# A fourth tile of 512-column matmuls in the selection turns, and a new table that places 46 additions

## The chip, the cores and the metric

The kernel runs on one core of one Trainium2 chip. The metric is the device time of one execution in microseconds (us). Five engines work beside each other, each through its own list of instructions, and they meet at semaphores: TensorE (PE in the rows; PEld is its weight load), VectorE (DVE), ScalarE (ACT), GpSimd (POOL) and SyncE (SP), which here issues the DMAs.

## The reference, cut to what matters

One transformer-like block for 256 tokens of width 1024: three mixers (a state-space scan, block attention, retention), an output projection, and then a layer of 16384 experts with product keys. The change lies in the expert layer:

```python
q = (hf @ w_q).reshape(t, PEER_HEADS, 2, PEER_QDIM // 2)
sc = jnp.einsum('thcd,hcnd->thcn', q, sub_keys)
sv, si = lax.top_k(sc, PEER_TOPK)                  # the selection
fs, fp = lax.top_k(cand_s, PEER_TOPK)
gates = jax.nn.softmax(fs, axis=-1)
act = jax.nn.gelu(jnp.einsum('cd,chkd->chk', xc, ue))
out = jnp.einsum('chk,chkd->cd', gc * act, ve)
```

Each token picks 16 experts per head by two top-16 searches. The kernel computes the gelu of all 16384 experts for all 256 tokens instead of gathering, and then multiplies by gates that are zero for experts not picked.

## The kernel before, in words

**Tiles and turns.** The 16384 experts are 128 tiles of 128 experts. A turn has four tiles (`UN` = 4, called slots 0 to 3 here), so there are 32 turns of the first product (`keys_turn`) and then 32 of the second (`values_turn`). A tile (t, s) is slot s of turn t. Each tile of the first product contracts over 1024 = 8 blocks of 128 (two halves of four).

**Precision in halves.** Every float operand is split into a high part (fp32r) and a low part. ScalarE makes the high part of the weights (`w_hi<-raw`, L1673, two instructions of 512 columns per tile), GpSimd makes the low part (`w_lo<-raw,w_hi`, L1840, two per tile). Three products are wanted: high by high, high by low, low by high.

**Narrow and wide tiles.** A narrow tile makes the three products as three matmuls of 256 columns for each of the 8 blocks (`halves_product`, L450 to L452), all added up in one PSUM region. A wide tile joins the token operand's high and low parts side by side (`h_both`) and makes one matmul of 512 columns (L763) and one of 256 (L765, and L762 for the last block). Its PSUM bank then holds two halves that have to be added: ScalarE copies the second half to SBUF (`con<-ps`, L1720, called the copy below), VectorE adds it to the first (`ps<-ps,con`, L836, called the addition), and ScalarE applies the gelu (`acts<-ps`, L1702). A narrow tile has the gelu alone. Two PSUM banks are used in turns, so a tile can start only when the gelu of the tile two before it is done (`act_ready`).

**Which tiles are wide.** Turns 0, 1, 12, 13, 14 and all those after are wide in all slots (but for slot 3 of the last turn). Turns 2 to 11 are wide in slots 0 to 2 only (`WIDE_SEL`). These are the turns beside which VectorE does the selection.

**The selection on VectorE.** It consists of 286 steps, counted by `did`, in two passes of 133 steps (128 tokens each) and a softmax. A pass is: 16 MAX8, 32 searches and replacements, 16 MAX8 and 16 searches over 128 keys (steps 1 to 80), a CAST (L1280), a COPY, a sum of 2048 columns; 8 MAX8, 16 searches and replacements, 8 MAX8 and 8 searches (L1233) over 256 candidates (to step 123); then step 124, a subtraction of two SBUF tiles (L836, `routing<-routing`), 125 and 126, two TENSOR_SCALARs (L1289, L1290), 127, a CAST (L1292), and six operations of 2048 columns (steps 128 to 133). In the second pass 133 is to be added: L1289 is step 258, L1290 is 259, L1292 is 260.

**What sets the order.** Every engine works its list strictly in order. The order on VectorE is written by a table: after the steps named in `PART_STEPS` the next outstanding addition is put into VectorE's list (`next_part`). An addition that comes before its copy is done makes VectorE wait; one that comes after it makes ScalarE's gelu wait, and TensorE at last. After step 286 a copy of one column (L1322) tells TensorE that the gates are ready (`tok_ready`); TensorE waits for it after turn 13, ahead of the transposes of L794.

Of the kernel before, what the change touches and what calls it, by code (L numbers as in the profile page):

```python
# [67 lines left out]
UN = 4  # L68
# [3 lines left out]
G_TURN0 = TURNS - 1 - S // GT // UN  # L72
ROUTE_TURN = G_TURN0 - 1
EXP_TURN = G_TURN0 - 2
LOWEST = -3e38
WIDE_S, WIDE_SEL, WIDE_LAST = (0, 1, 2, 3), (0, 1, 2), (0, 1, 2)
SEL0, SEL1 = 2, EXP_TURN - 1
WIDE_TURNS = {0: 0, 1: 4, **{t: 8 + 3 * (t - SEL0) for t in range(SEL0, SEL1)}}
WIDE_TURNS |= {t: 8 + 3 * (SEL1 - SEL0) + UN * (t - SEL1) for t in range(SEL1, G_TURN0)}
WIDE_G0 = WIDE_TURNS[ROUTE_TURN] + UN  # L80
SEL_PARTS = [(t, s) for t in range(SEL0, ROUTE_TURN) for s in (WIDE_SEL if t < SEL1 else WIDE_S)]

PART_STEPS = (21, 30, 39, 62, 71, 80, 89, 95, 101, 115, 121, 126, 129, 130, 131, 135, 147, 156, 176, 185, 197, 215, 216, 223,
              236, 242, 249, 260, 261, 262, 264, 265, 266, 271, 276, 281)
WIDE_END = WIDE_G0 + S // GT

TWO_PI = 2 * np.pi
# [45 lines left out]
def build(nc, x, w_in, vecs, consts, rots, decay, mask, s5_b, s5_c, w_glu, w_out, w_q, keys, u_t, v, out, spill):  # L133
    with ExitStack() as ctx:
# [285 lines left out]
        def _(pe):  # L420
# [25 lines left out]
            def halves_product(dst, pairs, first, last):  # L446

                for i, (s_hi, s_lo, m_hi, m_lo) in enumerate(pairs):
                    end = last and i == len(pairs) - 1
                    pe.matmul(dst, s_hi, m_hi, start=first and i == 0, stop=False)  # L450
                    pe.matmul(dst, s_hi, m_lo, start=False, stop=False)  # L451
                    mm = pe.matmul(dst, s_lo, m_hi, start=False, stop=end)  # L452
                return mm
# [286 lines left out]
            def keys_turn(t, groups=None, first=False, first_group=False, wide=()):  # L740

                for s in range(UN):
                    if first and s == 0:
                        pe.wait_ge(scaled_ready, KC)
                    elif not (first and s < 2):
                        pe.wait_ge(act_ready, UN * t + s - 1)
                    for h in range(2):
                        if first and s == 0:
                            pe.wait_ge(th_ready, TH0 + 2 * KC + 4 * h + 4)
                            pe.wait_ge(tl_ready, TL0 + 2 * KC + 4 * h + 4)  # L750
                        pe.wait_ge(lo_ready, TAIL + 8 * t + 2 * s + h + 1)
                        slot = 2 * (s % 2) + h
                        pairs = [(w_hi[:, slot, k * P:(k + 1) * P], w_lo[:, slot, k * P:(k + 1) * P],
                                  h_hi[:, H2_PLACE[4 * h + k], :], h_lo[:, H2_PLACE[4 * h + k], :]) for k in range(4)]
                        if s not in wide:
                            halves_product(ps[:, s % 2, 0:S], pairs, h == 0, h == 1).then_inc(half_used, 1)
                            continue
                        for k, (s_hi, s_lo, m_hi, _) in enumerate(pairs):
                            both = h_both[:, H2_PLACE[4 * h + k]].rearrange("p a t -> p (a t)")
                            end = h == 1 and k == 3  # L760
                            if end:
                                pe.matmul(ps[:, s % 2, 0:S], s_lo, m_hi, start=False, stop=False)  # L762
                            mm = pe.matmul(ps[:, s % 2, :], s_hi, both, start=(h == 0 and k == 0), stop=end)  # L763
                            if not end:
                                mm = pe.matmul(ps[:, s % 2, 0:S], s_lo, m_hi, start=False, stop=False)  # L765
                        mm.then_inc(half_used, 1)
                    if groups is not None:
                        g = groups + s
                        pe.wait_ge(hot_ready, g + 1)
                        if not (first_group and s < 2):  # L770
                            pe.wait_ge(group_done, g - 1)
                        for q in range(GT):
                            mm = pe.matmul(ps[:, 4 + 2 * (s % 2) + q // 2, (q % 2) * 2 * NKEY:(q % 2 + 1) * 2 * NKEY],  # L773
                                           hot_j[:, s % 2, q, :], hot_gate[:, s % 2, q].rearrange("p a i -> p (a i)"),
                                           start=True, stop=True)
                        mm.then_inc(group_psum, 1)

            keys_turn(0, first=True, wide=WIDE_S)
            pe.wait_ge(keys_in, 16)
            pe.wait_ge(pq_ready, PH)  # L780
            key_scores(0)
            keys_turn(1, wide=WIDE_S)
            pe.wait_ge(sc_ready, 4)
            key_scores(1)
            with pe.Fori(2, EXP_TURN - 1) as t:
                keys_turn(t, wide=WIDE_SEL)
            pe.wait_ge(sc_ready, 8)
            keys_turn(EXP_TURN - 1, wide=WIDE_S)
            keys_turn(EXP_TURN, wide=WIDE_S)

            pe.wait_ge(tok_ready, 1)
            for t in range(TT):
                for a in range(3):
                    mm = pe.transpose(ps[:, 4 + t, a * P:(a + 1) * P], rows[:, t, a, :], ident)  # L794
            mm.then_inc(route_psum, 1)
            keys_turn(ROUTE_TURN, wide=WIDE_S)
            pe.wait_ge(route_low, TT)
            keys_turn(G_TURN0, groups=0, first_group=True, wide=range(UN))
            with pe.Fori(G_TURN0 + 1, TURNS - 1) as t:
# [27 lines left out]
        def _(dve):  # L827
# [115 lines left out]
            wide = lambda a: a.unsqueeze(2).to_broadcast([P, S5_T, 32])  # L943
# [304 lines left out]
                tt(ps[:, s % 2, 0:S], ps[:, s % 2, 0:S], low_out, ALU.add).then_inc(added, 1)  # L1248

            def add_parts(t):  # L1250
                for s in WIDE_S:
                    add_part(WIDE_TURNS[t] + s, s)

            queries(1)
# [4 lines left out]
            def next_part():  # L1259

                t, s = SEL_PARTS[sel_added[0]]
                add_part(WIDE_TURNS[t] + s, s)
                sel_added[0] += 1

            def did(ins):

                ch.did(ins)
                if ch.n - sel_first in PART_STEPS:
                    next_part()
# [52 lines left out]
            V.tensor_copy(top2[:, 0, 0:1], top2[:, 0, 1:2]).then_inc(tok_ready, 1)  # L1322
            while sel_added[0] < len(SEL_PARTS):
                next_part()
            add_part(WIDE_TURNS[ROUTE_TURN], 0)
            for t in range(TT):
# [3 lines left out]
            dve.wait_ge(route_low, TT)  # L1330
            add_part(WIDE_TURNS[ROUTE_TURN] + 1, 1)
            add_part(WIDE_TURNS[ROUTE_TURN] + 2, 2)
# [87 lines left out]
        def _(act):  # L1420
# [271 lines left out]
            def key_scores(t, b):  # L1692
                act.wait_ge(sc_psum, t + 1)
                A.activation(sc[:, t, b // 2, 4 * (b % 2):4 * (b % 2) + 4, :],
                             ps[:, 4 + b, :].rearrange("p (h n) -> p h n", h=4), ACT.Copy,
                             scale=rstd[:, t:t + 1]).then_inc(sc_ready, 1)
# [7 lines left out]
            def keys_turn(t, groups=None, first=False, first_group=False, extra=None, wide=(), wide_0=0, carried=None):  # L1704
                for s in range(UN):
                    n = UN * t + s
                    high(n + 1, (s + 1) % UN, t + (s + 1) // UN)
                    if extra is not None:
                        extra(s)
                    if groups is not None and not (first_group and s == 0):  # L1710
                        group_out(groups + s - 1, (s - 1) % 2)
                    if s == 0 and carried is not None:
                        act.wait_ge(added, carried)
                        gelu(t - 1, UN - 1, first)
                    if s - 1 in wide:
                        act.wait_ge(added, wide_0 + s)
                        gelu(t, s - 1, first)
                    act.wait_ge(half_used, TAIL + 2 * n + 2)
                    if s in wide:
                        A.activation(low_out, ps[:, s % 2, S:2 * S], ACT.Copy).then_inc(part_ready, 1)  # L1720
                    else:
                        gelu(t, s, first)

            def wide_turn(t, **how):
                after = WIDE_TURNS[t] if t in (1, EXP_TURN, ROUTE_TURN) else None
                keys_turn(t, wide=WIDE_S, wide_0=WIDE_TURNS[t], carried=after, **how)

            def group_out(g, b):

# [9 lines left out]

            wide_turn(0, first=True, extra=last_queries)  # L1740
            wide_turn(1, extra=lambda s: key_scores(0, s))
            keys_turn(2, extra=lambda s: key_scores(1, s), wide=WIDE_SEL, wide_0=WIDE_TURNS[SEL0], carried=WIDE_TURNS[1] + UN)
            with act.Fori(3, EXP_TURN - 1) as t:
                keys_turn(t, wide=WIDE_SEL, wide_0=3 * t + (WIDE_TURNS[SEL0] - 3 * SEL0))
            wide_turn(EXP_TURN - 1)

            def route_rows(s):
# [15 lines left out]
            with act.Fori(G_TURN0 + 1, TURNS - 1) as t:  # L1763
                keys_turn(t, groups=UN * t - UN * G_TURN0, wide=range(UN), wide_0=UN * t + (WIDE_G0 - UN * G_TURN0),
                          carried=UN * t + (WIDE_G0 - UN * G_TURN0))
# [149 lines left out]
```

## Time and profile before

| | us |
|---|---|
| median of 3 runs | 901.53 |
| lowest and highest | 901.40, 901.64 |
| the profiled execution | 901.37 |
| its span, first to last instruction | 899.6 |

The profiled execution is 0.16 us from the median. Between its span and its time lie 1.8 us that no instruction of the profile fills. The page gives the busy time of each engine as a share of the span; the chain says which engine's work, followed back from the last instruction, the end hung on. TensorE's granted clock is 1.0 (the upper level, 2.4 GHz) in all slices. The selection turns lie at about 180 to 294 us.

### The profile page before, as it was taken

The numbers are of one execution on the slowest core, as the hardware profiler recorded it, in microseconds if no ns is written. First come the engines' busy times: TensorE is split into PE (matmuls) and PEld (weight loads), VectorE is DVE, ScalarE is ACT, GpSimd is POOL, SyncE is SP. The second block draws the span as 40 slices with busy tenths as digits, with TensorE's granted clock in tenths as the row PEclk, the third lists the DMA queues.
The fourth block names the chain that finished last, engine by engine and source line by source line (L and its number), as shares of the span: only waits on it lengthen the run. The fifth ranks groups of instructions, "written<-read, shape, count | busy, mean of one in ns | idle before, by whom it ended". The sixth has DMA issues, their size and how long they took to land.

```text
span 899.6 us, 18356 instructions
## 1 busy us (share of the span) xinstructions
PE 891.8 (99%) x4842; PEld 761.1 (85%) x4842; DVE 744.5 (83%) x1697; ACT 576.9 (64%) x1182; POOL 426.4 (47%) x342
## 2 busy tenths in 40 slices
PE   8999999999999999999999999999999999999998
PEld 5877888899999888888888888888888888888886
DVE  7979535199999859999999988888888888888886
ACT  7759566665555567777777776565656565655563
POOL 5875288889999987777777772000000000000000
PEclk9999999999999999999999999999999999999999
DMA  9835050566666665555565657766667677666663
GB/s 335 296 108 188 1 211 23 197 204 231 232 233 231 229 221 207 202 199 209 189 219 186 216 184 262 246 236 235 244 243 244 238 243 244 233 240 247 242 239 128
DMA packets 67755, 191.52 MB, mean 213 GB/s; under 512 B 6672, under 2 KB 8592, under 8 KB 67728
## 3 DMA queue, kind: packets, MB, share of 16 engines
q1 hardware_dynamic: 67440, 191.09, 60.6%
q8 instruction: 13, 0.21, 0.1%
q10 hardware_dynamic: 288, 0.10, 0.0%
q14 instruction: 14, 0.11, 0.0%
HBM read 173.86 MB, written 17.30 MB: 212 GB/s over the span
## 4 chain that ended last, share of the span: by engine, by line
PE 94%; DVE 3%; DMA 1%; ACT 0%; SPq 0%; issue 0%; DVEq 0%
PE ps L763 24%; PE ps L450 16%; PE ps L451 16%; PE ps L452 16%; PE ps L765 11%; PE ps L773 3%; PE ps L717 2%; PE ps L762 2%; DMA routing<-in_w_in 1%; DVE ps L836 1%; PE ps L719 1%; DVE routing L836 1%; DVE ps L1014 1%; PE ps L736 0%; PE ps L611 0%; PE ps L442 0%
## 5 line engine op out<-in xcount | busy, mean ns | idle before, releaser
L1673 ACT ACTIVATE w_hi<-raw 128x512 fp32r<-128x512 f32 x512 | 308.2, 628 | 136.1 <-PE ps L452 135.3
L1840 POOL TENSOR_TENSOR w_lo<-raw,w_hi 128x512 fp32r<-128x512 f32 x256 | 327.1, 1300 | 67.2 <-ACT w_hi L1673 66.4
L763 PE MATMUL ps<-h_both,w_hi 128*128 128x512 f32 x936 | 331.5, 394 | 0.0
L765 PE MATMUL ps<-h_both,w_lo 128*128 128x256 f32 x819 | 229.4, 280 | 0.0
L836 DVE TENSOR_TENSOR w_lo<-raw,w_hi 128x512 fp32r<-128x512 f32 x256 | 177.3, 693 | 57.1 <-ACT w_hi L1673 41.8
L763 PEld LDWEIGHTS ps<-h_both,w_hi 128*128 128x128 f32 x936 | 173.8, 188 | 31.1 <-issue 0.2
L450 PE MATMUL ps<-w_hi,hot_gate 128*128 128x512 f32 x512 | 199.2, 389 | 0.0
L452 PE MATMUL ps<-w_hi,hot_gate 128*128 128x512 f32 x512 | 199.2, 389 | 0.0
L451 PE MATMUL ps<-w_lo,hot_gate 128*128 128x512 f32 x512 | 199.2, 389 | 0.0
L765 PEld LDWEIGHTS ps<-h_both,w_lo 128*128 128x128 f32 x819 | 154.7, 189 | 1.1
L1720 ACT ACTIVATE con<-ps 128x256 f32<-128x256 f32 x117 | 45.0, 385 | 108.4 <-PE ps L763 108.4
L450 PEld LDWEIGHTS ps<-w_hi,hot_gate 128*128 128x128 f32 x512 | 96.1, 188 | 20.1
L451 PEld LDWEIGHTS ps<-w_lo,hot_gate 128*128 128x128 f32 x512 | 96.1, 188 | 19.9
L452 PEld LDWEIGHTS ps<-w_hi,hot_gate 128*128 128x128 f32 x512 | 96.1, 188 | 19.9
L1805 POOL TENSOR_TENSOR w_lo<-routing,w_hi 128x512 fp32r<-128x512 f32 x72 | 91.9, 1297 | 40.2 <-ACT w_hi L1440 39.2
L1352 DVE SCALAR_TENSOR_TENSOR hot_gate<-ps,route_t 128x256 fp32r<-128x256 f32 x256 | 105.6, 475 | 0.0
L836 DVE TENSOR_TENSOR route_t<-acts,routing 128x256 f32<-128x256 f32 x128 | 81.3, 635 | 0.0
L836 DVE TENSOR_TENSOR ps<-ps,con 128x256 f32<-128x256 f32 x117 | 49.9, 426 | 37.8 <-ACT con L1720 37.2
L1702 ACT ACTIVATE acts<-ps 128x256 f32<-128x256 f32 x128 | 48.8, 381 | 20.4 <-PE ps L452 11.7
L836 DVE TENSOR_TENSOR routing<-routing,ps 128x512 f32 (+3 forms) x74 | 51.3, 700 | 11.8 <-ACT routing L1679 6.1
L1440 ACT ACTIVATE w_hi<-routing 128x512 fp32r<-128x512 f32 x70 | 42.6, 628 | 22.9 <-PE ps L452 19.6
L1770 ACT ACTIVATE hot_gate<-route_t 128x256 fp32r<-128x256 f32 x128 | 53.5, 418 | 2.3 <-DVE route_t L836 2.3
(242 smaller groups left out, 1090.2 us busy)
## 6 DMA issues: line engine op xcount, KB each, us to landing
raw<-in_u_t SPq DMA_DIRECT2D x128, 512.0 KB, 4.0
raw<-in_v SPq DMA_DIRECT2D x128, 512.0 KB, 3.3
act_spill<-acts SPq DMA_DIRECT2D x62, 256.0 KB, 2.2
acts<-act_spill SPq DMA_DIRECT2D x62, 256.0 KB, 3.4
routing<-in_w_in SPq DMA_DIRECT2D x4, 2048.0 KB, 11.9
routing<-in_w_out SPq DMA_DIRECT2D x2, 2048.0 KB, 7.6
routing<-in_w_q SPq DMA_DIRECT2D x2, 2048.0 KB, 7.7
routing<-in_w_in SPq DMA_DIRECT2D x2, 1024.0 KB, 10.7
```

The lines of the kernel that those rows point to most:

```text
L450: pe.matmul(dst, s_hi, m_hi, start=first and i == 0, stop=False)
L451: pe.matmul(dst, s_hi, m_lo, start=False, stop=False)
L452: mm = pe.matmul(dst, s_lo, m_hi, start=False, stop=end)
L763: mm = pe.matmul(ps[:, s % 2, :], s_hi, both, start=(h == 0 and k == 0), stop=end)
L765: mm = pe.matmul(ps[:, s % 2, 0:S], s_lo, m_hi, start=False, stop=False)
L836: return V.tensor_tensor(out_, a, b, op)
L1352: ins = V.scalar_tensor_tensor(hot_gate[:, s % 2, q], iota_p.unsqueeze(1).to_broadcast([P, 2, NKEY]), route_t[:, 0, one], route_t[:, 2:4, ...
L1673: A.activation(w_hi[:, 2 * (s % 2) + h, :], raw[:, s, h * HALF:(h + 1) * HALF], ACT.Copy)\
L1702: A.activation(acts[:, s, :], ps[:, s % 2, 0:S], ACT.Gelu_apprx_tanh).then_inc(act_ready, 1)
L1770: A.activation(a_hi[:, s, :], weighted[:, s % 2, :], ACT.Copy).then_inc(wh_ready, 1)
L1805: G.tensor_tensor(w_lo[:, m % 4, :], w_ring[n % W_SLOTS][:, k, :], w_hi[:, m % 4, :].bitcast(F32), ALU.subtract).then_inc(lo_ready, 1)
L1840: G.tensor_tensor(w_lo[:, slot, :], raw[:, s, h * HALF:(h + 1) * HALF], w_hi[:, slot, :].bitcast(F32), ALU.subtract).then_inc(lo_ready, 1)
```

## The change

Slot 3 of turns 2 to 11 becomes wide. TensorE's `keys_turn` and ScalarE's `keys_turn` get all four slots, ScalarE carries the gelu of slot 3 into the next turn as it did in the all-wide turns, and VectorE gets ten more additions. With them the list of additions during the selection grows from 38 to 48, of which the table places 46 (36 before); the last two follow the selection's end as before.

```diff
-WIDE_S, WIDE_SEL, WIDE_LAST = (0, 1, 2, 3), (0, 1, 2), (0, 1, 2)
+WIDE_LAST = (0, 1, 2)
-SEL_PARTS = [(t, s) for t in range(SEL0, ROUTE_TURN) for s in (WIDE_SEL if t < SEL1 else WIDE_S)]
+SEL_PARTS = [(t, s) for t in range(SEL0, ROUTE_TURN) for s in range(UN)]
-PART_STEPS = (21, 30, 39, 62, 71, 80, ..., 115, 121, 126, 129, 130, 131, 135, ..., 249, 260, 261, 262, 264, ..., 276, 281)
+PART_STEPS = (21, 31, 40, 49, 61, 71, ..., 114, 120, 127, 128, 129, 130, 131, 132, 134, ..., 254, 258, 261, 262, 263, ..., 277, 282)
...
             with pe.Fori(2, EXP_TURN - 1) as t:
-                keys_turn(t, wide=WIDE_SEL)
+                keys_turn(t, wide=range(UN))
...
             with act.Fori(3, EXP_TURN - 1) as t:
-                keys_turn(t, wide=WIDE_SEL, wide_0=3 * t + (WIDE_TURNS[SEL0] - 3 * SEL0))
+                keys_turn(t, wide=range(UN), wide_0=UN * t, carried=UN * t)
```

The lines of the new kernel are numbered 1 to 2 lower than those of the old one (L836 becomes L835, L763 becomes L762).

On TensorE, in the loop over turns 3 to 11, the second half of slot 3 reads before (L450 to L452 are the three products of a narrow tile, `h_both` the token operand):

```order
L450 MATMUL ps<-h_both,w_hi 128x256
L451 MATMUL ps<-h_both,w_hi 128x256
L452 MATMUL ps<-h_both,w_lo 128x256
L450 MATMUL ps<-h_both,w_hi 128x256
L451 MATMUL ps<-h_both,w_hi 128x256
L452 MATMUL ps<-h_both,w_lo 128x256
```

and now, at the same place:

```order
L762 MATMUL ps<-h_both,w_hi 128x512
L764 MATMUL ps<-h_both,w_lo 128x256
L762 MATMUL ps<-h_both,w_hi 128x512
L764 MATMUL ps<-h_both,w_lo 128x256
L762 MATMUL ps<-h_both,w_hi 128x512
L764 MATMUL ps<-h_both,w_lo 128x256
```

Three matmuls of 256 columns per block became one of 512 and one of 256.

On VectorE, the end of the first pass (steps 115 to 130) before; MAX_INDEX is the search, `ps<-ps,con` an addition:

```order
215 L836 TENSOR_TENSOR ps<-ps,con 128x256
216 L1233 MAX_INDEX routing<-routing 128x8 x6
217 L836 TENSOR_TENSOR ps<-ps,con 128x256
218 L1233 MAX_INDEX routing<-routing 128x8 x2
219 L836 TENSOR_TENSOR routing<-routing 128x128
220 L1289 TENSOR_SCALAR routing<-routing 128x128
221 L1290 TENSOR_SCALAR routing<-routing 128x128
222 L836 TENSOR_TENSOR ps<-ps,con 128x256
223 L1292 CAST routing<-routing 128x256
224 L836 TENSOR_TENSOR ps<-routing,ps 128x2048
225 L836 TENSOR_TENSOR routing<-ps,routing 128x2048
226 L836 TENSOR_TENSOR ps<-ps,con 128x256
```

and now:

```order
222 L835 TENSOR_TENSOR ps<-ps,con 128x256
223 L1232 MAX_INDEX routing<-routing 128x8 x3
224 L835 TENSOR_TENSOR routing<-routing 128x128
225 L1288 TENSOR_SCALAR routing<-routing 128x128
226 L1289 TENSOR_SCALAR routing<-routing 128x128
227 L1291 CAST routing<-routing 128x256
228 L835 TENSOR_TENSOR ps<-ps,con 128x256
229 L835 TENSOR_TENSOR ps<-routing,ps 128x2048
230 L835 TENSOR_TENSOR ps<-ps,con 128x256
231 L835 TENSOR_TENSOR routing<-ps,routing 128x2048
```

The addition of tile (5, 2) stood ahead of the CAST and now stands behind it, and there is an addition behind each of the 2048-column operations that follow.

On VectorE, the same place of the second pass before:

```order
306 L836 TENSOR_TENSOR ps<-ps,con 128x256
307 L1233 MAX_INDEX routing<-routing 128x8 x7
308 L836 TENSOR_TENSOR routing<-routing 128x128
309 L1289 TENSOR_SCALAR routing<-routing 128x128
310 L1290 TENSOR_SCALAR routing<-routing 128x128
311 L1292 CAST routing<-routing 128x256
312 L836 TENSOR_TENSOR ps<-ps,con 128x256
313 L836 TENSOR_TENSOR ps<-routing,ps 128x2048
314 L836 TENSOR_TENSOR ps<-ps,con 128x256
```

and now:

```order
318 L835 TENSOR_TENSOR ps<-ps,con 128x256
319 L1232 MAX_INDEX routing<-routing 128x8 x2
320 L835 TENSOR_TENSOR routing<-routing 128x128
321 L1288 TENSOR_SCALAR routing<-routing 128x128
322 L835 TENSOR_TENSOR ps<-ps,con 128x256
323 L1289 TENSOR_SCALAR routing<-routing 128x128
324 L1291 CAST routing<-routing 128x256
325 L835 TENSOR_TENSOR ps<-routing,ps 128x2048
326 L835 TENSOR_TENSOR ps<-ps,con 128x256
```

The addition of tile (11, 0) moved from behind the CAST to between the two TENSOR_SCALARs, and the one of tile (10, 3) (row 318) is new.

## Rows read from the trace of the kernel before

**Rows 1.** Page, part 1 (busy us, share of span, instructions) and part 4 (chain)

```profile
PE 891.8 (99%) x4842; PEld 761.1 (85%) x4842; DVE 744.5 (83%) x1697; ACT 576.9 (64%) x1182; POOL 426.4 (47%) x342
...
PE 94%; DVE 3%; DMA 1%; ACT 0%; SPq 0%; issue 0%; DVEq 0%
```

**Rows 2.** Table by stage: turns 2-11, turn 12 (start:end width, busy us per engine)

```profile
183.44:296.54 113.10, 113.10 (x722) 102.47 (x721) 109.38 (x417) 68.09 (x153) 101.21 (x80) 1.00 0.68 232
296.54:307.77 11.23, 11.23 (x65) 9.86 (x65) 9.56 (x16) 6.79 (x16) 10.21 (x9) 1.00 0.64 212
```

**Rows 3.** Timeline, TensorE: start us, length us, line, operation; narrow slot 3 of turn 2

```profile
189.09 0.28 PE L450 MATMUL ps<-h_both,w_hi 128*128 128x256 f32 x1
189.21 0.28 PE L451 MATMUL ps<-h_both,w_hi 128*128 128x256 f32 x1
...
191.97 0.40 PE L763 MATMUL ps<-h_both,w_hi 128*128 128x512 f32 x1
192.20 0.28 PE L765 MATMUL ps<-h_both,w_lo 128*128 128x256 f32 x1
192.32 0.40 PE L763 MATMUL ps<-h_both,w_hi 128*128 128x512 f32 x1
```

**Rows 4.** Waits, 180 to 316 us: total us, times, longest us

```profile
POOL w_lo L1840 <- ACT w_hi L1673: 14.2, 40, 2.4
...
DVE ps L836 <- ACT con L1720: 4.3, 14, 0.7
```

**Rows 5.** Timeline, TensorE, last matmul of a tile and first of the next

```profile
197.35 0.63 PE L763 MATMUL ps<-h_both,w_hi 128*128 128x512 f32 x2
```

**Rows 6.** Timeline, ScalarE, copies, weight splits and gelus

```profile
197.78 0.39 ACT L1720 ACTIVATE con<-ps 128x256 f32<-128x256 f32 x1 [1.09 <-PE ps L763]
...
220.38 0.39 ACT L1720 ACTIVATE con<-ps 128x256 f32<-128x256 f32 x1 [1.13 <-PE ps L763]
...
223.16 0.38 ACT L1720 ACTIVATE con<-ps 128x256 f32<-128x256 f32 x1 [1.09 <-PE ps L763]
...
228.85 0.38 ACT L1720 ACTIVATE con<-ps 128x256 f32<-128x256 f32 x1 [1.25 <-PE ps L763]
229.13 1.15 ACT L1673 ACTIVATE w_hi<-raw 128x512 fp32r<-128x512 f32 x2
230.62 0.38 ACT L1702 ACTIVATE acts<-ps 128x256 f32<-128x256 f32 x1 [0.34 <-DVE ps L836]
```

**Rows 7.** Timeline, GpSimd

```profile
221.36 2.60 POOL L1840 TENSOR_TENSOR w_lo<-raw,w_hi 128x512 fp32r<-128x512 f32 x2 [0.28 <-ACT w_hi L1673]
224.15 2.59 POOL L1840 TENSOR_TENSOR w_lo<-raw,w_hi 128x512 fp32r<-128x512 f32 x2 [0.19 <-ACT w_hi L1673]
...
283.82 5.19 POOL L1840 TENSOR_TENSOR w_lo<-raw,w_hi 128x512 fp32r<-128x512 f32 x4 [0.47 <-ACT w_hi L1673]
...
311.82 2.60 POOL L1840 TENSOR_TENSOR w_lo<-raw,w_hi 128x512 fp32r<-128x512 f32 x2 [0.25 <-ACT w_hi L1673]
```

**Rows 8.** Timeline, VectorE, end of the first pass

```profile
220.79 0.43 DVE L836 TENSOR_TENSOR ps<-ps,con 128x256 f32<-128x256 f32 x1
221.14 0.08 DVE L1233 MATCH_VALUE_LOAD routing<-routing 128x8 f32 x1
...
221.54 0.07 DVE L1233 MATCH_VALUE_LOAD routing<-routing 128x8 f32 x1
...
222.05 0.76 DVE L836 TENSOR_TENSOR routing<-routing 128x128 f32<-128x128 f32 x1
222.73 1.31 DVE L1289 TENSOR_SCALAR routing<-routing 128x128 uint32<-128x128 uint32 x1
223.97 0.21 DVE L1290 TENSOR_SCALAR routing<-routing 128x128 uint32<-128x128 uint32 x1
224.10 0.42 DVE L836 TENSOR_TENSOR ps<-ps,con 128x256 f32<-128x256 f32 x1
224.44 1.15 DVE L1292 CAST routing<-routing 128x256 f32<-128x256 uint32 x1
225.62 2.30 DVE L836 TENSOR_TENSOR ps<-routing,ps 128x2048 f32<-128x2048 f32 x1
227.96 2.29 DVE L836 TENSOR_TENSOR routing<-ps,routing 128x2048 f32<-128x2048 f32 x1
230.16 0.42 DVE L836 TENSOR_TENSOR ps<-ps,con 128x256 f32<-128x256 f32 x1
```

**Rows 9.** Timeline, VectorE, the same place of the second pass

```profile
283.46 0.29 DVE L836 TENSOR_TENSOR routing<-routing 128x128 f32<-128x128 f32 x1
283.67 0.22 DVE L1289 TENSOR_SCALAR routing<-routing 128x128 uint32<-128x128 uint32 x1
283.80 0.22 DVE L1290 TENSOR_SCALAR routing<-routing 128x128 uint32<-128x128 uint32 x1
284.06 1.27 DVE L1292 CAST routing<-routing 128x256 f32<-128x256 uint32 x1
```

**Rows 10.** Timeline, VectorE, end of the selection, and TensorE's transposes behind it

```profile
313.19 1.38 DVE L836 TENSOR_TENSOR routing<-routing 128x128 f32<-128x128 f32 x1
314.61 0.15 DVE L1322 COPY routing<-routing 128x1 f32<-128x1 f32 x1
...
316.25 0.82 PE L794 MATMUL ps<-con,routing 128*128 128x128 f32 x6
```

More of the change, by code:

```diff
@@ L75 @@
 LOWEST = -3e38
-WIDE_S, WIDE_SEL, WIDE_LAST = (0, 1, 2, 3), (0, 1, 2), (0, 1, 2)
+WIDE_LAST = (0, 1, 2)
 SEL0, SEL1 = 2, EXP_TURN - 1
-WIDE_TURNS = {0: 0, 1: 4, **{t: 8 + 3 * (t - SEL0) for t in range(SEL0, SEL1)}}
-WIDE_TURNS |= {t: 8 + 3 * (SEL1 - SEL0) + UN * (t - SEL1) for t in range(SEL1, G_TURN0)}
+WIDE_TURNS = {t: UN * t for t in range(G_TURN0)}
 WIDE_G0 = WIDE_TURNS[ROUTE_TURN] + UN
-SEL_PARTS = [(t, s) for t in range(SEL0, ROUTE_TURN) for s in (WIDE_SEL if t < SEL1 else WIDE_S)]
-PART_STEPS = (21, 30, 39, 62, 71, 80, 89, 95, 101, 115, 121, 126, 129, 130, 131, 135, 147, 156, 176, 185, 197, 215, 216, 223,
-              236, 242, 249, 260, 261, 262, 264, 265, 266, 271, 276, 281)
+SEL_PARTS = [(t, s) for t in range(SEL0, ROUTE_TURN) for s in range(UN)]
+PART_STEPS = (21, 31, 40, 49, 61, 71, 80, 83, 88, 95, 101, 107, 114, 120, 127, 128, 129, 130, 131, 132, 134, 146, 156, 165,
+              175, 184, 197, 206, 214, 216, 222, 228, 235, 241, 248, 254, 258, 261, 262, 263, 264, 265, 266, 272, 277, 282)
 WIDE_END = WIDE_G0 + S // GT
@@ L776, in keys_turn @@
                         mm.then_inc(group_psum, 1)
-            keys_turn(0, first=True, wide=WIDE_S)
+            keys_turn(0, first=True, wide=range(UN))
             pe.wait_ge(keys_in, 16)
@@ L781, in _ @@
             key_scores(0)
-            keys_turn(1, wide=WIDE_S)
+            keys_turn(1, wide=range(UN))
             pe.wait_ge(sc_ready, 4)
@@ L785, in _ @@
             with pe.Fori(2, EXP_TURN - 1) as t:
-                keys_turn(t, wide=WIDE_SEL)
+                keys_turn(t, wide=range(UN))
             pe.wait_ge(sc_ready, 8)
-            keys_turn(EXP_TURN - 1, wide=WIDE_S)
-            keys_turn(EXP_TURN, wide=WIDE_S)
+            keys_turn(EXP_TURN - 1, wide=range(UN))
+            keys_turn(EXP_TURN, wide=range(UN))
             pe.wait_ge(tok_ready, 1)
@@ L795, in _ @@
             mm.then_inc(route_psum, 1)
-            keys_turn(ROUTE_TURN, wide=WIDE_S)
+            keys_turn(ROUTE_TURN, wide=range(UN))
             pe.wait_ge(route_low, TT)
@@ L1250, in add_parts @@
             def add_parts(t):
-                for s in WIDE_S:
+                for s in range(UN):
                     add_part(WIDE_TURNS[t] + s, s)
@@ L1724, in wide_turn @@
             def wide_turn(t, **how):
-                after = WIDE_TURNS[t] if t in (1, EXP_TURN, ROUTE_TURN) else None
-                keys_turn(t, wide=WIDE_S, wide_0=WIDE_TURNS[t], carried=after, **how)
+                keys_turn(t, wide=range(UN), wide_0=WIDE_TURNS[t], carried=WIDE_TURNS[t] if t else None, **how)
             def group_out(g, b):
@@ L1741, in _ @@
             wide_turn(1, extra=lambda s: key_scores(0, s))
-            keys_turn(2, extra=lambda s: key_scores(1, s), wide=WIDE_SEL, wide_0=WIDE_TURNS[SEL0], carried=WIDE_TURNS[1] + UN)
+            keys_turn(2, extra=lambda s: key_scores(1, s), wide=range(UN), wide_0=WIDE_TURNS[SEL0], carried=WIDE_TURNS[1] + UN)
             with act.Fori(3, EXP_TURN - 1) as t:
-                keys_turn(t, wide=WIDE_SEL, wide_0=3 * t + (WIDE_TURNS[SEL0] - 3 * SEL0))
+                keys_turn(t, wide=range(UN), wide_0=UN * t, carried=UN * t)
             wide_turn(EXP_TURN - 1)
```

## The prediction

> **What bounds the kernel now.** I read the busy shares and the chain first [rows 1]: TensorE is busy for 99% of the span and holds 94% of the chain, so the end moves with TensorE's list alone, by what its instructions cost and by what it is made to wait. Then I read the table by stage for the stretch that the change touches [rows 2]: over the ten selection turns TensorE is busy in all of the 113.10 us, so before the change it never waits there. VectorE (109.38) and GpSimd (101.21) are nearly as full. The view of waits [rows 4] says what VectorE has to spare: it waits 14 times, 4.3 us in all, for ScalarE's copy, and GpSimd waits 40 times, 14.2 us in all, for the split weights, about once per tile. So TensorE is the bound, VectorE runs at its pace with some 4 us of slack, and what can go wrong is an addition that comes too late.
>
> **What TensorE gains.** The columns are the same: 24 matmuls of 256 columns are 6144, 8 of 512 and 8 of 256 are 6144 as well. What differs is the spacing. In the narrow tile matmuls start 0.12 us apart (189.09, 189.21), and the tile takes 191.97 - 189.09 = 2.88 us [rows 3]. In the wide one a pair starts every 0.35 us (191.97 to 192.32), 8 x 0.35 = 2.80. By stages: the ten turns with one narrow tile take 113.10 / 10 = 11.31 us, the all-wide turn 12 takes 11.23, which is 2.81 a tile [rows 2]. The difference is 0.08 a turn, ten times: **-0.8 us**. The bounds are -0.7 (2.88 less 2.81) and, if each of the 80 weight loads that vanish freed all of its time, -12.6: the loads are busy for 761.1 us over 4842 of them [rows 1], 0.157 each. Matmuls that start 0.12 us apart [rows 3] while a load takes more than that show that the loads overlap, so I take -0.8.
>
> **What the other engines get.** ScalarE gets ten copies of 0.38 us (3.8 us; it is busy 68.09 of 113.10 us [rows 2], and its order in slot 3 becomes that of the slots before it). VectorE gets ten additions, each holding its list for 0.35 us (220.79 to 221.14 [rows 8]): 3.5 us, less than the 4.3 us of waits, so as a sum they fit. The last additions and the end of the selection stay within their slack: VectorE's signal at 314.61 lasts to 314.76, TensorE comes to L794 at 316.25 [rows 10], 1.5 us later. The last placed addition, of tile (13, 1), moves one step later, and its tile comes earlier with TensorE, so this slack stays. DMAs don't change; the results of slots 2 and 3 are stored somewhat later in the turn, since the gelu of slot 3 now follows the next turn's first split; the waits of this stretch are for engines, none of the large ones for a DMA. What decides is each addition's place.
>
> **How late an addition may be.** Let c be the start of a tile's copy. The copy takes 0.39 us and the addition can start 0.03 us behind it, at c + 0.42. ScalarE then splits the next weights; the gelu starts 0.46 us after the addition's start if that is later (230.16 to 230.62) and takes 0.38, so it ends 0.84 us after the addition's start [rows 6, 8]. The tile's last matmul starts at c - 0.43 (197.35 against 197.78) and the next tile's first 0.24 later, at c - 0.19 [rows 5, 6]. The tile after that reuses the bank and wants to start at c - 0.19 + 2.81 = c + 2.62. So the addition must start by c + 1.78, 1.36 us after it could; each microsecond beyond it is one on TensorE. The latest before is at 230.16 for the copy of 228.85, which is 0.89 us behind c + 0.42 [rows 6, 8], and TensorE did not wait.
>
> **What makes VectorE late.** Three operations at the end of a pass take far longer in one place than in the other: the subtraction 0.76 against 0.29 us, L1289 1.31 against 0.22, and the CAST 1.15 and 1.27 [rows 8, 9]. Beside GpSimd's rows the reason shows: GpSimd's pair of 221.36 consists of two operations of 1.30 us. The subtraction of 222.05 ends when the first does (222.66), L1289 ends when the second does (223.96), L1290 at 223.97 falls into GpSimd's gap and takes 0.21, and the CAST ends just after 224.15 + 1.30 = 225.45. In the second pass the subtraction, L1289 and L1290 all start before 283.82, when GpSimd starts again, and are short; the CAST of 284.06 ends with GpSimd's operation [rows 7, 9]. The 1.38 us of the product at 313.19 end with the pair of 311.82 too [rows 7, 10]. So these forms wait for GpSimd's operation in progress, and where GpSimd has its next one ready, one such form passes between two of GpSimd's. GpSimd's pair starts at c + 0.98 (221.36 against 220.38), its first operation ends at c + 2.28, the pair at c + 3.58, and the next pair starts at c + 2.81 + 0.98 = c + 3.79: the gap is 0.2 us.
>
> The Trainium skill ("SBUF — State Buffer", section "Who interferes with whom") states the same as a lock: VectorE with two SBUF inputs, or in a two-port mode (copy, cast, tensor_scalar), and GpSimd exclude each other for whole instructions. Without that rule nothing speaks against the new table and the sum would be -0.8; with it the two stalls below are to be added. The trace agrees with it at the four places just read.
>
> **First pass, tile (5, 2).** Let c be the copy of tile (5, 1). Its addition is now behind step 120, at c + 0.42. VectorE goes on at c + 0.77, three searches follow (0.40, 0.40 and 0.51 by the starts 221.14, 221.54, 222.05 [rows 8]), and the subtraction is asked for at c + 2.08: before c + 2.28, so it ends there, L1289 ends at c + 3.58, L1290 starts at c + 3.59 in the gap. The CAST follows 0.26 later (283.80 to 284.06 [rows 9]), at c + 3.85. GpSimd has started at c + 3.79. So the CAST ends at about c + 5.1, and the addition of (5, 2), which stood ahead of it before and now stands behind it, starts at c + 5.2. Its limit is c + 2.81 + 1.78 = c + 4.59: **+0.6 us**. Behind it two 2048-column operations of 2.20 us (227.96 to 230.16 [rows 8]), each with an addition of 0.35, run at 2.55 a tile against 2.81, so the lateness falls by 0.26 a tile and costs nothing more.
>
> **Second pass, tile (11, 1).** Let c be the copy of tile (10, 3). Addition at c + 0.42, two searches, subtraction asked for at c + 0.77 + 0.40 + 0.51 = c + 1.68, inside GpSimd's first operation. It ends at c + 2.28, L1289 at c + 3.58. The addition of (11, 0) is now here: c + 3.59 to c + 3.94, which covers the gap. L1290 comes at c + 3.94, GpSimd started at c + 3.79: L1290 ends at c + 5.09, and the CAST behind the second operation at c + 6.39. The 2048-column comparison starts 0.17 later (225.45 to 225.62 [rows 7, 8]) and takes 2.20, so the addition of (11, 1) starts at c + 8.76. Its limit is c + 5.62 + 1.78 = c + 7.40: **+1.4 us**. Before, the three forms fell ahead of GpSimd's start, and the addition ahead of this comparison.
>
> No row shows TensorE held by a gelu, so what a restart costs can't be read. I bound it by 0 and by the 0.19 us from a tile's end to ScalarE's copy, the same kind of release the other way round [rows 5, 6], and take 0, since TensorE's next matmul stands ready in its list; the two stalls could thus be 0.4 longer in all.
>
> **The sum.** -0.8 + 0.6 + 1.4 = +1.2 us, against the profiled execution 901.37 + 1.2 = 902.6, against the median 901.53 + 1.2 = 902.7. I forecast **902.7 us**. A difference under 0.2% (1.8 us) is about what a measurement of this kernel can tell from no change, and by that this is no change.
>
> **The rivals.**
>
> *No stall: 900.7 us.* The holds by GpSimd don't fall as worked out, and TensorE keeps its 0.8 us. For it: TensorE is never held before, with one addition already 0.89 us late, and VectorE's holds vary between passes. Against it: GpSimd's gap is 0.2 us in 2.8, so a form that it holds rarely misses it.
>
> *One stall only: 901.3 to 902.1 us.* -0.8 + 0.6 = -0.2, if L1290 slips ahead of GpSimd in the second pass, by 0.15 us: then one hold goes, the limit is overrun by some 0.1 to 0.3 and the sum is -0.8 + 0.6 + 0.3 = +0.1 at most, 901.3 to 901.6. Or -0.8 + 1.4 = +0.6 if the CAST of the first pass slips ahead by its 0.06 us: 902.1.
>
> *Slower, by a hold more: 904.0 us.* In the first pass L1290 has to be in GpSimd's gap, 0.2 us wide. If the subtraction comes 0.2 us later than worked out (after c + 2.28), it takes the place of L1289, L1289 that of L1290, and L1290 misses the gap. Then another 1.30 us is put on the addition of (5, 2): the stall is 1.9, the sum -0.8 + 1.9 + 1.4 = +2.5. It decides from that 0.2 us on. For it: three more additions ahead of this point, of tiles (2, 3), (3, 3) and (4, 3), each 0.35 us of VectorE's time. Against it: VectorE waits for the copy of nearly every tile and so starts afresh.
>
> *The wide tile saves more than its spacing: under 899.7 us.* Weight loads would have to be what TensorE is short of; the 0.12 us spacing speaks against it.
>
> **How the numbers follow.** Forecast 0.48; no stall 0.18; one stall only 0.16; a hold more 0.14; more saved 0.04. The forecast, no stall and one stall lie within 0.2% of before, 0.82, of which I give 0.02 to the outer sides. Faster 0.05, same 0.80, slower 0.15. The range goes from 900.6, just below the case without a stall, to 904.0, the case with one hold more; outside are the larger gain and half of the slow case, some 0.15.
>
> **What would show it.** In the profile after: the windows of ten turns at 11.23 us each but for two longer ones; the matmuls of slot 3 at 0.35 a pair; a wait of TensorE for the gelu ahead of tile (6, 0), some 0.6 us, and ahead of (11, 3), some 1.4 us; the last CAST of each pass, and in the second pass both TENSOR_SCALARs, at some 1.2 us; no wait ahead of the transposes. The prediction is wrong if TensorE isn't held in these turns, or is held at other tiles, or if the ten turns' matmuls cost more or less than 11.15 to 11.30 a turn without a wait.

## The result and the profile after

| | median us | lowest to highest | runs |
|---|---|---|---|
| before | 901.19 | 900.58 to 901.64 | 15 |
| changed | 902.89 | 902.51 to 903.80 | 15 |

The ratio is 1.0021, with a 95% interval from 1.0014 to 1.0028: the change costs 1.7 us (1.2 were forecast, 902.7 us). The forecast held such a difference too small to tell from no change; fifteen runs of each kernel do tell it.

The page of the changed kernel, parts 1 and 4, answers to [rows 1]:

```profile
PE 891.7 (99%) x4762; PEld 756.7 (84%) x4762; DVE 749.6 (83%) x1707; ACT 579.3 (64%) x1192; POOL 426.2 (47%) x342
...
PE 88%; DVE 10%; ACT 1%; DMA 1%; issue 0%; POOL 0%; SPq 0%; DVEq 0%
```

80 matmuls are gone, as counted, and TensorE is as busy as before in all. What is new is that the chain which ended last now runs over VectorE for 10% of the span, not 3%. It enters VectorE's list at two additions and follows it back from there, from 226.0 to 218.5 us and from 292.3 to 244.6 us. This says where to look, in the selection turns, but not what VectorE costs there: the share is far more than the 1.7 us at stake.

The table by stage, with the ten selection turns in the first row (from the boundary of slots 0 and 1 of turn 2 to that of turn 12, as in [rows 2]) and turn 12 in the second:

```profile
184.13:298.91 114.78, 112.94 (x641) 98.24 (x641) 113.27 (x427) 71.04 (x163) 101.10 (x80) 1.00 0.68 227
298.91:310.11 11.20, 11.20 (x66) 9.83 (x65) 10.76 (x18) 6.79 (x16) 10.20 (x9) 1.00 0.74 234
```

The ten turns take 114.78 us against 113.10, so 1.68 us more, and TensorE, busy in all of it before, is now idle for 1.8 us of it. This matches the medians' 1.7. The two profiled spans differ by 2.3 us (901.9 against 899.6), because the profiled execution of the changed kernel took 903.73 us, 0.84 above its median; the other 0.69 lies before turn 2, which begins anywhere between 183.1 and 184.5 us in the nine profiles of this study, whatever the edit. So from here on the ten turns are the meter: they don't see what happens at the start. Each such number is one profile. How far it can be trusted is not measured by itself; two kernels that should not differ in it, before and before with the indices in PSUM, have 113.10 and 113.08.

TensorE's waits in the stretch are two. Its timeline around the first, ahead of tile (6, 0), and around the second, ahead of (11, 3); in brackets the idle time and what ended it:

```profile
226.08 0.39 PE L762 MATMUL ps<-h_both,w_hi 128*128 128x512 f32 x1
227.00 0.49 PE L762 MATMUL ps<-h_both,w_hi 128*128 128x512 f32 x1 [0.53 <-ACT acts L1701]
227.34 0.28 PE L764 MATMUL ps<-h_both,w_lo 128*128 128x256 f32 x1
227.45 0.40 PE L762 MATMUL ps<-h_both,w_hi 128*128 128x512 f32 x1
...
291.58 0.39 PE L762 MATMUL ps<-h_both,w_hi 128*128 128x512 f32 x1
293.28 0.49 PE L762 MATMUL ps<-h_both,w_hi 128*128 128x512 f32 x1 [1.31 <-ACT acts L1701]
293.61 0.28 PE L764 MATMUL ps<-h_both,w_lo 128*128 128x256 f32 x1
```

The brackets say 0.53 and 1.31, less than is lost. Matmuls of 512 columns start 0.24 us apart from tile to tile, here 0.92 and 1.70: that is 0.68 and 1.46. The first pair after each wait takes 0.45 instead of 0.35 (227.00 to 227.45). So each wait costs 0.1 more: 0.78 and 1.56, together 2.34 us. From 113.10 + 2.34 = 115.44 to 114.78 the wide tiles then give back 0.66.

What ended the waits is ScalarE's gelu, started late; its copies of tiles (5, 1) and (10, 3), from which the prediction counts, are the first row of each pair:

```profile
220.88 0.39 ACT L1719 ACTIVATE con<-ps 128x256 f32<-128x256 f32 x1 [1.09 <-PE ps L762]
...
226.49 0.38 ACT L1701 ACTIVATE acts<-ps 128x256 f32<-128x256 f32 x1 [1.37 <-DVE ps L835]
...
283.59 0.39 ACT L1719 ACTIVATE con<-ps 128x256 f32<-128x256 f32 x1 [1.12 <-PE ps L762]
...
292.77 0.38 ACT L1701 ACTIVATE acts<-ps 128x256 f32<-128x256 f32 x1 [2.15 <-DVE ps L835]
```

The view of waits also has one of 1.6 us of the weight load ahead of (11, 3), put down to GpSimd's low parts. But GpSimd's pair before it ends at 290.18 + 2.52 = 292.70, and the load starts at 293.28 with the matmul: the gelu, done at 293.15, came last there.

VectorE and GpSimd at the first place. VectorE in the end of the first pass, to be read against [rows 8]:

```profile
221.30 0.43 DVE L835 TENSOR_TENSOR ps<-ps,con 128x256 f32<-128x256 f32 x1
...
222.95 0.35 DVE L835 TENSOR_TENSOR routing<-routing 128x128 f32<-128x128 f32 x1
223.22 1.32 DVE L1288 TENSOR_SCALAR routing<-routing 128x128 uint32<-128x128 uint32 x1
224.46 0.21 DVE L1289 TENSOR_SCALAR routing<-routing 128x128 uint32<-128x128 uint32 x1
224.70 1.41 DVE L1291 CAST routing<-routing 128x256 f32<-128x256 uint32 x1
226.04 0.42 DVE L835 TENSOR_TENSOR ps<-ps,con 128x256 f32<-128x256 f32 x1
```

GpSimd in the same stretch:

```profile
221.86 2.59 POOL L1838 TENSOR_TENSOR w_lo<-raw,w_hi 128x512 fp32r<-128x512 f32 x2 [0.23 <-ACT w_hi L1672]
224.68 2.57 POOL L1838 TENSOR_TENSOR w_lo<-raw,w_hi 128x512 fp32r<-128x512 f32 x2 [0.23 <-ACT w_hi L1672]
```

The CAST asks at 224.70, 0.02 us after GpSimd has started its next pair. It lasts 1.41 us, to 226.11, about the end of GpSimd's first instruction at 224.68 + 1.30 = 225.98, and the addition behind it starts at 226.04. The addition before all this, at 221.30, starts 0.03 us behind the end of its copy (220.88 + 0.39 = 221.27): VectorE had not fallen behind up to there. The same holds in the second pass (284.01 against 283.98).

VectorE at the same place of the second pass, to be read against [rows 9]:

```profile
284.01 0.43 DVE L835 TENSOR_TENSOR ps<-ps,con 128x256 f32<-128x256 f32 x1
...
285.26 0.89 DVE L835 TENSOR_TENSOR routing<-routing 128x128 f32<-128x128 f32 x1
286.07 1.32 DVE L1288 TENSOR_SCALAR routing<-routing 128x128 uint32<-128x128 uint32 x1
287.32 0.42 DVE L835 TENSOR_TENSOR ps<-ps,con 128x256 f32<-128x256 f32 x1
287.65 1.11 DVE L1289 TENSOR_SCALAR routing<-routing 128x128 uint32<-128x128 uint32 x1
288.79 1.28 DVE L1291 CAST routing<-routing 128x256 f32<-128x256 uint32 x1
290.11 2.30 DVE L835 TENSOR_TENSOR ps<-routing,ps 128x2048 f32<-128x2048 f32 x1
292.31 0.43 DVE L835 TENSOR_TENSOR ps<-ps,con 128x256 f32<-128x256 f32 x1
```

GpSimd beside it:

```profile
284.72 5.20 POOL L1838 TENSOR_TENSOR w_lo<-raw,w_hi 128x512 fp32r<-128x512 f32 x4 [0.41 <-ACT w_hi L1672]
```

Its four instructions end at 286.02, 287.32, 288.62 and 289.92, and the four forms end at 286.15, 287.39, 288.76 and 290.07: one behind each. The subtraction and the two TENSOR_SCALARs took 0.29, 0.22 and 0.22 before and are now all held; the CAST was held before too (1.27). The addition of tile (11, 1) starts at 292.31, 2.7 us after its copy (289.20 to 289.59) is done.

The wait ahead of the transposes did not come: they start at 318.60, and VectorE's signal is issued at 316.97.

### The profile page after: what moved, and what is told of

It reads as the page before. It is cut to its first block, busy times and chain, and to the rows that moved or that the text cites. A ratio compares the mean times of both kernels' runs of the same rounds, so it can differ in the third digit from the quotient of the medians.

```text
span 901.9 us, 18129 instructions
## 1 busy us (share of the span) xinstructions
PE 891.7 (99%) x4762; PEld 756.7 (84%) x4762; DVE 749.6 (83%) x1707; ACT 579.3 (64%) x1192; POOL 426.2 (47%) x342
## 4 chain that ended last, share of the span: by engine, by line
PE 88%; DVE 10%; ACT 1%; DMA 1%; issue 0%; POOL 0%; SPq 0%; DVEq 0%
PE ps L762 22%; PE ps L449 15%; PE ps L450 15%; PE ps L451 15%; PE ps L764 10%; PE ps L772 3%; DVE ps L835 2%; PE ps L716 1%; PE ps L761 1%; DVE routing L1232 1%; DVE routing L835 1%; DVE routing L1225 1%; DVE routing L1226 1%; DMA xs<-in_x 1%; DVE routing L1229 1%; PE ps L718 1%
## 5 line engine op out<-in xcount | busy, mean ns | idle before, releaser
L762 PE MATMUL ps<-h_both,w_hi 128*128 128x512 f32 x1016 | 357.7, 395 | 1.8 <-ACT acts L1701 1.8
L764 PE MATMUL ps<-h_both,w_lo 128*128 128x256 f32 x889 | 249.1, 280 | 0.0
L835 DVE TENSOR_TENSOR w_lo<-raw,w_hi 128x512 fp32r<-128x512 f32 x256 | 177.3, 693 | 54.0 <-ACT w_hi L1672 39.5
L762 PEld LDWEIGHTS ps<-h_both,w_hi 128*128 128x128 f32 x1016 | 187.5, 188 | 36.2 <-POOL w_lo L1838 1.6
L450 PE MATMUL ps<-w_lo,hot_gate 128*128 128x512 f32 x512 | 199.2, 389 | 0.0
L764 PEld LDWEIGHTS ps<-h_both,w_lo 128*128 128x128 f32 x889 | 167.9, 189 | 1.9
L1719 ACT ACTIVATE con<-ps 128x256 f32<-128x256 f32 x127 | 48.8, 385 | 113.4 <-PE ps L762 113.4
L450 PEld LDWEIGHTS ps<-w_lo,hot_gate 128*128 128x128 f32 x512 | 96.1, 188 | 19.8
L835 DVE TENSOR_TENSOR route_t<-acts,routing 128x256 f32<-128x256 f32 x128 | 81.3, 635 | 3.2 <-PE ps L451 2.7
L835 DVE TENSOR_TENSOR ps<-ps,con 128x256 f32<-128x256 f32 x127 | 53.9, 424 | 34.4 <-ACT con L1719 34.2
L835 DVE TENSOR_TENSOR routing<-routing,ps 128x512 f32 (+3 forms) x74 | 51.3, 700 | 11.9 <-ACT routing L1678 6.1
```

Source lines behind the costliest of these rows:

```text
L835: return V.tensor_tensor(out_, a, b, op)
```

## The experiments

Seven kernels were run, in two groups. All ten-turn times are between the same two boundaries.

**Take away what holds the operations.** In the changed kernel, the tile that the TENSOR_SCALARs write and the CAST reads lies in PSUM. The CAST's result `ab_f` stays in SBUF. (The words put on record speak of both tiles; one was moved, which is enough to give each of the three operations one SBUF operand.)

```diff
-        ab = tab[:, 1024:1280].bitcast(U32).rearrange("p (c h k) -> p c h k", c=2, h=PH)
+        ab = ps[:, 2, 256:512].bitcast(U32).rearrange("p (c h k) -> p c h k", c=2, h=PH)
```

> The changed kernel with its table untouched; the two index tiles that the TENSOR_SCALARs write and the CAST reads lie in PSUM, so that these three operations have one SBUF operand. Theory (they are held by GpSimd's operation in progress, the additions behind them come late, TensorE waits): the three are short (under 0.45 us) wherever they fall, no wait of TensorE at tiles (6, 0) and (11, 3), the ten turns between the first slot boundaries of turns 2 and 12 take 114.78 - 0.78 - 1.56 = 112.4 us, the time is 0.7 us below the kernel before (ratio 0.9993). Rival (the operations are long for a reason of VectorE's own, such as its instruction fetch or the integer types): they stay at 1.1 to 1.4 us, the ten turns at 114.8, the ratio at 1.002.

Measured: 900.75 us against 901.27 before, ratio 0.9993 (0.9984 to 1.0002), and no wait of TensorE. The table by stage for the ten turns, and VectorE in the first pass:

```profile
183.67:296.24 112.57, 112.57 (x641) 98.46 (x641) 109.82 (x427) 70.71 (x163) 101.13 (x80) 1.00 0.69 231
...
222.77 0.28 DVE L1288 TENSOR_SCALAR ps<-routing 128x128 uint32<-128x128 uint32 x1
222.97 0.28 DVE L1289 TENSOR_SCALAR ps<-routing 128x128 uint32<-128x128 uint32 x1
223.28 0.42 DVE L1291 CAST routing<-ps 128x256 f32<-128x256 uint32 x1
223.65 0.43 DVE L835 TENSOR_TENSOR ps<-ps,con 128x256 f32<-128x256 f32 x1
```

GpSimd's pairs in that profile:

```profile
221.40 2.60 POOL L1838 TENSOR_TENSOR w_lo<-raw,w_hi 128x512 fp32r<-128x512 f32 x2 [0.23 <-ACT w_hi L1672]
```

All three run within GpSimd's pair of 221.40 to 224.00 and take 0.28, 0.28 and 0.42 us. In the second pass the subtraction, whose two inputs are still in SBUF, is held as before, and the three behind it are not, though GpSimd is busy from 283.53 to 288.75:

```profile
284.08 0.90 DVE L835 TENSOR_TENSOR routing<-routing 128x128 f32<-128x128 f32 x1
284.90 0.28 DVE L1288 TENSOR_SCALAR ps<-routing 128x128 uint32<-128x128 uint32 x1
...
285.98 0.28 DVE L1289 TENSOR_SCALAR ps<-routing 128x128 uint32<-128x128 uint32 x1
286.30 0.42 DVE L1291 CAST routing<-ps 128x256 f32<-128x256 uint32 x1
```

```profile
283.53 5.22 POOL L1838 TENSOR_TENSOR w_lo<-raw,w_hi 128x512 fp32r<-128x512 f32 x4 [0.41 <-ACT w_hi L1672]
```

With the same table, the same engines and the same integer types the holds of these three are gone, and with them the waits: 112.57 us against the 112.4 of the theory. The rival (a reason of VectorE's own) is out.

**Control on the kernel before.** The same edit there.

> The kernel BEFORE with the two index tiles in PSUM. Control: its additions are all in time, so making the held operations short gains nothing: ten turns at 113.1 us, TensorE without a wait. If it came out near 112.5, the gain of the same edit in the changed kernel would not be the waits'.

Measured: 113.08 us (183.48 to 296.56), 901.26 us in one run, no wait of TensorE. Short operations gain nothing where no addition is late, so the 2.2 us that the edit takes off the changed kernel's ten turns are the waits'. And 113.08 - 112.57 = 0.5 us is what the ten wide tiles give with everything else alike.

**Move one addition, then the other, then both.** In the changed kernel's table:

```diff
-... 120, 127, 128, ...      add_126 and add_126_259
+... 120, 126, 128, ...
-... 254, 258, 261, ...      add_259 and add_126_259
+... 254, 259, 261, ...
```

> Only 127 to 126. Theory: the wait ahead of tile (6, 0) goes, a small one (0.3 with its restart) comes ahead of (6, 1), the one ahead of (11, 3) stays at 1.3: ten turns 114.78 - 0.78 + 0.3 = 114.3 us. Rival (one late addition is repaid later on, the two waits are not separate): ten turns at 113.0 or at 114.8.

Measured: 114.14 us (183.13 to 297.27), one run at 902.21. One wait is left in the view, of 1.3 us, ahead of (11, 3); ahead of (6, 1) two matmuls take 0.92 us instead of 0.63, a loss of 0.3 that the view doesn't show.

> Only 258 to 259. Theory: the wait ahead of tile (11, 3) shrinks from 1.3 us to under 0.3, because only the CAST is held and not the second TENSOR_SCALAR, the one ahead of (6, 0) stays at 0.5: ten turns 114.78 - 1.56 + 0.3 = 113.5 us. Rival: ten turns at 114.8, the wait moves to another tile.

Measured: 113.48 us (183.55 to 297.03), one run at 901.89. The one wait in the view is of 0.5 us, ahead of (6, 0). The second TENSOR_SCALAR of the second pass is at 0.22 us again, right behind the first, so it is not held, as expected. Ahead of (11, 3) two matmuls take 1.01 us instead of 0.63: 0.4 us are still lost there.

> The changed kernel with two numbers of the table moved: 127 to 126 (addition of (5, 2) ahead of the CAST of the first pass) and 258 to 259 (addition of (11, 0) behind both TENSOR_SCALARs of the second pass). Theory: the operations are still held, but (5, 2) starts at c + 3.7, in time; the comparison behind the CAST now makes the next addition, (5, 3), late by 0.06 us beyond its limit, and (11, 1) likewise. Each costs 0.1 and a restart of 0.2: the ten turns take 112.4 + 0.6 = 113.0, as the kernel before (113.1), ratio 1.000. Rival (TensorE's waits come from GpSimd's low parts or ScalarE's splits, not from these additions): 114.8, ratio 1.002.

Measured: 113.04 us, 901.15 us against 901.27, ratio 1.000 (0.9991 to 1.0009). The view of waits shows none, but TensorE's timeline around the boundary of tiles (6, 0) and (6, 1) does:

```profile
227.85 0.28 PE L761 MATMUL ps<-h_both,w_lo 128*128 128x256 f32 x1
227.97 0.92 PE L762 MATMUL ps<-h_both,w_hi 128*128 128x512 f32 x2
228.72 0.28 PE L764 MATMUL ps<-h_both,w_lo 128*128 128x256 f32 x1
```

The two matmuls of 512 columns across the boundary take 0.92 us where [rows 5] has 0.63. So a small wait hides as a long matmul: 0.3 us, which fits a limit overrun by 0.06, 0.13 for the release and 0.1 for the restart. The same stands once more in the second pass. The two edits change the ten turns by 0.64 and 1.30, and together by 1.74, where 1.94 would be the sum: the waits are separate but for 0.2 us.

**Make the wait in the kernel before.** The narrow fourth tile, no new addition, one number of its table:

```diff
-... 121, 126, 129, ...
+... 121, 127, 129, ...
```

> The kernel BEFORE, with its fourth tile still of 256 columns, and one number of its table moved from 126 to 127: the addition of (5, 2) stands behind the CAST of the first pass. Theory (the place behind a held operation makes the wait, whatever the tiles are): the CAST is held until 225.45 in the clock of the run before, the addition starts at 225.5, its limit is 223.16 + 1.78 + 0.07 = 225.0, so TensorE waits 0.5 us ahead of tile (6, 0) and loses 0.23 with the restart; the ten turns take 113.1 + 0.7 = 113.8 us, the time is 0.7 us above before (ratio 1.0008). Rival (the wide fourth tile and its ten additions are what fills VectorE up): no wait, 113.1 us.

Measured: 902.36 us against 901.28, ratio 1.0011 (1.0001 to 1.0020); ten turns 113.75 us (184.45 to 298.20), 0.65 more. The medians differ by 1.1 us, with an interval that reaches from 0.1 to 1.8. VectorE and then TensorE:

```profile
224.98 0.21 DVE L1290 TENSOR_SCALAR routing<-routing 128x128 uint32<-128x128 uint32 x1
225.23 1.37 DVE L1292 CAST routing<-routing 128x256 f32<-128x256 uint32 x1
226.52 0.42 DVE L836 TENSOR_TENSOR ps<-ps,con 128x256 f32<-128x256 f32 x1
```

```profile
226.72 0.28 PE L452 MATMUL ps<-h_both,w_lo 128*128 128x256 f32 x1
227.49 0.49 PE L763 MATMUL ps<-h_both,w_hi 128*128 128x512 f32 x1 [0.49 <-ACT acts L1702]
```

The place of one addition makes the wait, without any wide tile.

**Halve GpSimd's instructions.** In turns 0 to 12 of the changed kernel:

```diff
-                        G.tensor_tensor(w_lo[:, slot, :], raw[...], w_hi[...], ALU.subtract).then_inc(lo_ready, 1)
+                        n = HALF // parts
+                        for i in range(parts):
+                            ins = G.tensor_tensor(w_lo[:, slot, i * n:(i + 1) * n], raw[...], w_hi[...], ALU.subtract)
+                        ins.then_inc(lo_ready, 1)
```

> The changed kernel, table untouched; in turns 0 to 12 GpSimd makes each low part in two instructions of 256 columns instead of one of 512. Theory (a form waits for the end of GpSimd's instruction in progress, whole instructions take turns): each hold is at most half as long, 0.7 us instead of 1.3; (5, 2) then starts at c + 4.5 against its limit of c + 4.59, (11, 1) at c + 6.9 against c + 7.40, TensorE has no wait or one under 0.3 us, the ten turns take 112.6 to 112.9 us. If two instructions of 256 columns take clearly longer than one of 512, GpSimd itself holds TensorE back, which would show as a wait for its low parts. Rival (they share the port's bandwidth, so that the length of GpSimd's instructions does not matter): holds of 1.1 to 1.4 us as before, ten turns at 114.8.

Measured: 902.86 us in one run, ten turns 113.64 us (184.45 to 298.09). The view of waits has TensorE waiting for no gelu any more, and the 1.3 us ahead of (11, 3) are gone. A small wait is left ahead of (6, 0): the addition of (5, 2) starts at 226.16, 4.63 us behind the copy of (5, 1) (221.53), just beyond the limit of 4.59, and two matmuls at 226.73 take 0.89 us. VectorE's first pass, and GpSimd beside it:

```profile
224.02 0.76 DVE L1288 TENSOR_SCALAR routing<-routing 128x128 uint32<-128x128 uint32 x1
224.70 0.78 DVE L1289 TENSOR_SCALAR routing<-routing 128x128 uint32<-128x128 uint32 x1
225.52 0.73 DVE L1291 CAST routing<-routing 128x256 f32<-128x256 uint32 x1
```

```profile
218.30 9.92 POOL L1840 TENSOR_TENSOR w_lo<-raw,w_hi 128x256 fp32r<-128x256 f32 x14
```

The holds are half as long, 0.73 to 0.78 us, as GpSimd's instructions are (9.92 / 14 = 0.71). That speaks for whole instructions that take turns, and against a shared bandwidth. The stage came out 0.7 us or more above the theory for the reason that the expectation names as a possibility: four instructions of 0.71 are 2.84 us a tile against TensorE's 2.81, where two of 1.30 are 2.60, so that GpSimd is now itself the bound (113.64 / 40 = 2.84); TensorE's weight loads wait 8 times for its low parts by the view, 1.6 us in all, one of them ahead of (6, 0). As a remedy it is worthless, as a test it is clear.

In short:

| kernel | ten turns, us | TensorE waits ahead of |
|---|---|---|
| before | 113.10 | none |
| changed | 114.78 | (6, 0), (11, 3) |
| changed, 127 to 126 | 114.14 | (6, 1) little, (11, 3) |
| changed, 258 to 259 | 113.48 | (6, 0), (11, 3) little |
| changed, both | 113.04 | two little ones |
| changed, indices in PSUM | 112.57 | none |
| before, indices in PSUM | 113.08 | none |
| before, 126 to 127 | 113.75 | (6, 0) |
| changed, GpSimd in halves | 113.64 | low parts, 8 times; (6, 0) little |

The version with the indices in PSUM is the fastest of all: 0.5 us below the kernel before by the medians and by the stage, though its interval (0.9984 to 1.0002) just takes in 1.

## Why the prediction was right

*The bound and the slack.* Right. TensorE's list alone decides, and nothing downstream gave back what the ten turns lost.

*How late an addition may be.* Right to 0.15 us. The limit of 1.78 us behind the copy's start was worked out without a row in which TensorE waits. Now there are two: the matmul comes 0.96 and 0.97 us behind the late addition's start (226.04 to 227.00, 292.31 to 293.28) and wanted to come at 226.32 and 291.82, so the limits were c + 4.48 and c + 7.26 where the prediction had c + 4.59 and c + 7.40. The addition of (5, 2) starts 5.16 us after the copy of (5, 1) (220.88), of which the prediction said 5.2, that of (11, 1) 8.72 us after the copy of (10, 3) (283.59), predicted 8.76. The subtraction was to be asked for at 2.08 and 1.68, and was at 2.07 and 1.67.

*Where luck helped.* Two things fell better than the working deserved. In the second pass GpSimd started 0.15 us later than worked out (c + 1.13, not c + 0.98), and the gap of 0.2 us behind its second instruction was not there: it ran four without a break, as it had in [rows 7] at 283.82. The two cancel, so 8.76 came out as 8.72. And in the first pass the whole stall hung on the CAST's missing a gap by 0.06 us; it missed it by 0.02 (224.70 against 224.68). It did so by 0.04 and 0.08 us in the profiles of the two other runs with this order, so it was no single accident, but a margin this small was not known to be safe.

*What makes VectorE late.* Right, and shown: by the PSUM version, by the halved instructions and by the holds at the places named (four in the second pass, the CAST in the first). The Trainium skill's rule ("SBUF — State Buffer", section "Who interferes with whom") that VectorE and GpSimd exclude each other for whole instructions is what these runs show from VectorE's side (1.3 us with GpSimd's instructions of 1.30, 0.75 with those of 0.71). That VectorE holds GpSimd as well no run here was made to show.

*Restart.* Wrong in size. The term was bounded by 0 and 0.19 and taken as 0. Measured: 0.13 us from the gelu's end to the next matmul (226.49 + 0.38 = 226.87, then 227.00) and 0.1 us in the first pair, 0.23 for each wait. The stalls were 0.78 and 1.56 instead of 0.6 and 1.4; this is 0.3 of the 0.5 us that are missing.

*What TensorE gains.* Wrong in size, -0.8 where it was -0.66 by the accounting and -0.5 by the PSUM version against its control. The prediction compared with turn 12, where VectorE has little to do and tiles take 2.80 (11.20 / 4 in the profile after); within the selection a wide tile mostly takes 2.82. The lower bound of -0.7, from 2.88 less 2.81, was the better term. Why tiles of one form take 2.79 in some places and 2.82 in others was not tried.

*The rivals.* No stall (900.7 us) is what the PSUM version measured, 900.75, but not the changed kernel. One hold more did not come: in the first pass the second TENSOR_SCALAR (L1290 before, L1289 after) kept its place in GpSimd's gap, at 224.46. What was said against that rival, that VectorE waits for the copy of nearly every tile, is more than [rows 4] shows: 14 waits for 36 placed additions. One stall only, by the second TENSOR_SCALAR of the second pass slipping ahead of GpSimd, was further off than its 0.15 us: it came 0.33 us behind GpSimd's third instruction (287.65 against 287.32). More saved by loads: 80 loads less freed 0.5 us, not 12.6.

## What to carry to other kernels

Where one engine's list is written out by a table that places short, urgent work between long steps, the table is only as good as the durations behind it, and the duration of an operation that another engine can hold depends on when it falls (0.22 or 1.32 us here). Put the urgent instruction ahead of such an operation, not behind it, or change the operation so that it can't be held (one operand in PSUM did it here). When work is moved into a stretch that is full, work out for each instruction the latest start at which nothing waits, and compare: two of 46 were late here, and they cost more than ten tiles gained.

## What the runs showed that was not expected

- A small wait of TensorE does not appear as idle time: two matmuls shown as one row take longer (0.92 or 1.01 us instead of 0.63, a loss of 0.3 and 0.4 us). The spacing of the tiles finds it, the view of waits does not.
- On GpSimd two instructions of 256 columns take 1.42 us, one of 512 takes 1.30: by these two an estimated 0.12 us per instruction that does not depend on its width, enough to make it the bound of this stage.
- A hold that decides over 0.8 us hung on 0.02 us in the profiled run. Whether it fell in each of the fifteen runs can't be told; without it the median would be some 902.89 - 0.78 = 902.1 us, and the lowest of them is 902.51.
